# Waits per reader in place of the meetings of all engines between joint projection, SSD, RWKV and output projection; four SSD norm multiplications on GpSimd

## The reference, cut to what matters

```python
z, xbc, dt, rw, gq, gk, gv, gd, og = _split(u @ w_in, IN_WIDTHS)      # joint projection
xbc = silu(dwconv_centred(xbc))                                       # per channel, 3 taps
y = unboth(_ssd_chunked(both(xs, xs), both(dt_f, dt_b), ...))         # SSD, both directions
y = y + ssd_d[:, None] * xs
y_ssd = _rmsnorm_groups(y * silu(z), ssd_norm_w, 256)                 # SSD norm
kk = kk / jnp.maximum(jnp.sqrt(jnp.sum(kk * kk, -1)), 1e-12)          # RWKV preparation
y = unboth(_rwkv7_scan(both(r, r), both(w_f, w_b), ...))              # RWKV, both directions
y_rwkv = (layernorm_heads(y) * lnx_w + lnx_b + bonus) * gate
y_gla = ...
y_mix = jnp.concatenate([y_ssd, y_rwkv, y_gla], axis=-1)
return y_mix @ w_out                                                  # output projection
```

## Time and profile before

| | us |
|---|---|
| runs, median | 2151.59 |
| runs, lowest and highest of three | 2148.78, 2156.02 |
| the profiled execution, its own time | 2151.16 |
| its span, first to last instruction | 2149.0 |
| TensorE busy | 1929.7 |
| DVE busy | 1028.0 |
| ACT busy | 623.6 |
| GpSimd busy | 188.2 |

### The profile page before, as it was taken

How to read it: one execution, slowest core, us unless ns; L and a number is a source line. 1 busy time by engine, 2 the same in 40 slices (tenths; PEclk the granted TensorE clock), 3 DMA queues, 4 the chain that set the end, 5 groups by cost and what they waited for, 6 DMA issues and landing times.

```text
span 2149.0 us, 33639 instructions
## 1 busy us (share of the span) xinstructions
PE 1929.7 (90%) x14454; PEld 1401.6 (65%) x14454; DVE 1028.0 (48%) x1414; ACT 623.6 (29%) x917; POOL 188.2 (9%) x207
## 2 busy tenths in 40 slices
PE   6878999899996999899997669769899999999992
PEld 5758999889985999665755569665344444444440
DVE  4665555555555677645465674654222111121116
ACT  4334333444444433310142332121111112111110
POOL 0000000000000000011100004001112112121213
PEclk9878999999998999999897789679999999999996
DMA  9213555544443767445410000054999898998886
GB/s 321 99 59 128 186 185 183 167 157 138 157 144 102 284 235 253 134 163 177 128 59 3 12 2 4 26 234 170 391 379 380 344 384 348 378 384 346 333 342 245
DMA packets 191892, 438.67 MB, mean 204 GB/s; under 512 B 24208, under 2 KB 145552, under 8 KB 162448
## 3 DMA queue, kind: packets, MB, share of 16 engines
q1 hardware_dynamic: 156336, 352.02, 44.1%
q0 software_dynamic: 23040, 43.05, 5.9%
q10 hardware_dynamic: 12384, 41.69, 5.0%
HBM read 501.68 MB, written 26.21 MB: 246 GB/s over the span
## 4 chain that ended last, share of the span: by engine, by line
PE 80%; DVE 11%; ACT 4%; DMA 3%; issue 2%; SPq 0%; POOL 0%; ACTq 0%; DVEq 0%; POOLq 0%
PE psum L346 29%; PE psum L3207 15%; PE psum L3228 8%; PE psum L1574 7%; PE psum L3178 4%; PE psum L1581 2%; PE psum L2559 2%; ACT w_hi L412 1%; DMA mem<-in_exp_w_dram 1%; DMA mem<-in_na_w_qkv_dram 1%; DVE w_lo L417 1%; DVE mem L3328 1%; PE psum L2543 1%; PE psum L576 1%; PE psum L2968 1%
## 5 line engine op out<-in xcount | busy, mean ns | idle before, releaser
L417 DVE TENSOR_TENSOR w_lo<-mem,w_hi 128x2048 fp32r<-128x2048 f32 x126 | 288.4, 2291 | 271.3 <-ACT w_hi L412 268.7
L346 PE MATMUL psum<-x_hi,w_hi 128*128 128x256 f32 x1216 | 352.1, 290 | 4.6 <-DVE x_lo L563 4.6
L3207 PE MATMUL psum<-mem 128*64 128x512 f32 x1536 | 342.6, 599 | 9.5 <-DMA mem<-in_exp_w_dram 9.4
L346 PE MATMUL psum<-x_hi,w_lo 128*128 128x256 f32 x1216 | 346.2, 285 | 0.0
L346 PE MATMUL psum<-x_lo,w_hi 128*128 128x256 f32 x1216 | 345.4, 284 | 0.0
L412 ACT ACTIVATE w_hi<-mem 128x2048 fp32r<-128x2048 f32 x126 | 241.4, 1919 | 209.8 <-PE psum L346 190.8
L3207 PEld LDWEIGHTS psum<-mem 128*64 128x64 f32 x1536 | 110.8, 138 | 233.3 <-issue 214.8
L346 PEld LDWEIGHTS psum<-x_hi,w_hi 128*128 128x128 f32 x1216 | 236.0, 194 | 11.2 <-DVE w_lo L417 5.0
L346 PEld LDWEIGHTS psum<-x_lo,w_hi 128*128 128x128 f32 x1216 | 239.6, 197 | 0.7
L346 PEld LDWEIGHTS psum<-x_hi,w_lo 128*128 128x128 f32 x1216 | 238.3, 196 | 0.0
L3228 PE MATMUL psum<-mem 128*64 128x512 f32 x768 | 177.0, 603 | 1.2 <-DVE mem L3279 1.0
(11 more groups left out here) (485 smaller groups left out, 2899.6 us busy)
## 6 DMA issues: line engine op xcount, KB each, us to landing
mem<-in_exp_w_dram SPq DMA_DIRECT2D x192, 1024.0 KB
mem<-in_dil_w_qkv_dram SPq DMA_DIRECT2D x36, 1024.0 KB, 5.2
mem<-in_ada_w_dram POOLq DMA_DIRECT2D x48, 512.0 KB, 4.5
y_rows<-mem ACTq DMA_DIRECT2D x48, 512.0 KB
mem<-in_ffn_w_gate_dram SPq DMA_DIRECT2D x22, 1024.0 KB, 5.3
mem<-in_ffn_w_up_dram SPq DMA_DIRECT2D x22, 1024.0 KB, 5.4
mem<-in_ffn_w_down_dram SPq DMA_DIRECT2D x22, 1024.0 KB, 4.8
mem<-in_w_in_dram SPq DMA_DIRECT2D x13, 1024.0 KB, 5.7
```

The source lines that it names most:

```text
L346: ins = pe.matmul(out, lhs[a], rhs[b], start=start and k == 0, stop=stop and k == 2, **kw)
L417: dve.tensor_tensor(w_lo[n % SLOTS][:, 0, :], ring[:, n % SLOTS, :], w_hi_f[n % HI][:, 0, :], ALU.subtract).then_inc(S("w_split"), 1)
L3207: ins = pe.matmul(psum[r, up, :].rearrange("p (a n) -> p a n", a=2), xg[:, b % 2, c, x * P + 64 * e:x * P + 64 * e + 64], w_up[s][e][:, :, ...
```

## The change

The three meetings go. Instead, the instructions that need another engine's last work wait for that alone. The GpSimd program runs its parts without them. The four multiplications of the SSD norm go from DVE to GpSimd, whose result DVE waits for before it writes the end of RWKV. The scores of SSD go to bank 5. In ACT's program the root of the SSD norm and the load of `rk_masks` stand in the middle of `rwkv_prep_act`, and the three loads of the third meeting stand behind the first weight split. GpSimd's memset before the second FFN waits for `x_split` instead of `x_added`.

```diff
@@ wo_pe, wo_act
     def wo_pe(pe):
+        pe.wait_ge(S("gate_silu"), 4)
+        pe.wait_ge(S("rk_kr"), 3)
...
         hi_act(act, W_OUT)
+        act.wait_ge(S("rk_kr"), 3)
+        ln_load(act, 0)
+        act.dma_start(router_w, d["router_w_2"][0].rearrange("(p c) e -> p c e", p=P)).then_inc(S("router_in"), 16)
@@ block1_pool
-        pool.wait_ge(S("x_added"), NT * 3)
+        pool.wait_ge(S("x_split"), X_NO["ff1"] + KC)
         mod1_pool(pool)
@@ ssd_pe
-                ins = pe.matmul(bank(2, P, (2 * t + g) * P), xbcT[:, 4 + g, sd_tok(t)], xbcT[:, 6 + g, sd_tok(t)],
+                ins = pe.matmul(bank(5, P, (2 * t + g) * P), xbcT[:, 4 + g, sd_tok(t)], xbcT[:, 6 + g, sd_tok(t)],
...
+                if k == 0:
+                    pe.wait_ge(S("sd_turn_out"), 2 * t + 2)
                 pe.wait_ge(S("sd_xde_n"), m + 1)
...
             if k == 0:
+                pe.wait_ge(S("sd_turn_out"), 8)
                 rows(0)
@@ ssd_act
-        act.wait_ge(S("group_sums"), 2)
-        act.activation(stat[:, 1, 0:4], stat[:, 0, 0:4], ACT.Sqrt, scale=1 / 256, bias=ln_eps).then_inc(S("group_root"), 1)
@@ ssd_dve
+                else:
+                    dve.wait_ge(S("sd_turn_out"), 2 * t + 2)
                 xdt(t, dr, sd_xde[:, dr, :])
...
             if k == 0:
+                dve.wait_ge(S("sd_turn_out"), 8)
...
-            link(dve, "dve", dve.tensor_tensor(y, y, bank(5 + t), ALU.add))
+            dve.tensor_tensor(y, y, bank(5 + t), ALU.add).then_inc(S("sd_off"), 1)
+            dve.wait_ge(S("sd_off"), 5 + t)
...
-        dve.wait_ge(S("group_root"), 2)
-        link(dve, "dve", dve.reciprocal(stat[:, 3, 0:4], stat[:, 1, 0:4]))
+
+    def ssd_norm_pool(pool):
+
+        pool.wait_ge(S("sd_off"), 7)
         for t in range(NT):
-            y2 = y_mix[:, t, 0:512].rearrange("p (g e) -> p g e", g=2)
-            link(dve, "dve", dve.tensor_tensor(y2, y2, bc(stat[:, 3, 2 * t:2 * t + 2], 2, 256), ALU.mult))
-            link(dve, "dve", dve.tensor_tensor(y_mix[:, t, 0:512], y_mix[:, t, 0:512], vr("ssd_norm_w"), ALU.mult))
+            y, y2 = y_mix[:, t, 0:512], y_mix[:, t, 0:512].rearrange("p (g e) -> p g e", g=2)
+            link(pool, "pool", pool.tensor_tensor(y2, y2, bc(stat[:, 3, 2 * t:2 * t + 2], 2, 256), ALU.mult))
+            pool.tensor_tensor(y, y, vr("ssd_norm_w"), ALU.mult).then_inc(S("gate_silu"), 1)
@@ rwkv_prep_pe
+        pe.wait_ge(S("sd_off"), 5)
...
+        pe.wait_ge(S("sd_off"), 6)
         za(0)
@@ rwkv_prep_act
-        act.dma_start(rk_mask.rearrange("p d n i -> p (d n i)"), d["rk_masks"]).then_inc(S("rk_tri"), 16)
...
         act.activation(sq, psum[:, 4:6, :], ACT.Sqrt).then_inc(S("rk_norm"), 1)
+        act.wait_ge(S("group_sums"), 2)
+        act.activation(stat[:, 1, 0:4], stat[:, 0, 0:4], ACT.Sqrt, scale=1 / 256, bias=ln_eps).then_inc(S("group_root"), 1)
+        act.dma_start(rk_mask.rearrange("p d n i -> p (d n i)"), d["rk_masks"]).then_inc(S("rk_tri"), 16)
@@ rwkv_prep_dve
         link(dve, "dve", dve.reciprocal(sq, sq))
+        dve.wait_ge(S("group_root"), 2)
+        dve.reciprocal(stat[:, 3, 0:4], stat[:, 1, 0:4]).then_inc(S("sd_off"), 1)
@@ rwkv_end_dve
         dve.wait_ge(S("group_root"), 3)
+        dve.wait_ge(S("gate_silu"), 4)
...
-        link(dve, "dve", dve.tensor_tensor(y_mix[:, :, 512:768], yk, rk_g, ALU.mult))
+        dve.tensor_tensor(y_mix[:, :, 512:768], yk, rk_g, ALU.mult).then_inc(S("rk_kr"), 1)
@@ block2_pe, block2_act, block2_dve: each without its three calls
-        fence(pe, "mixed")
-        fence(pe, "ssd_done")
-        fence(pe, "rwkv_done")
@@ block2_act
-        ln_load(act, 0)
-        act.dma_start(router_w, d["router_w_2"][0].rearrange("(p c) e -> p c e", p=P)).then_inc(S("router_in"), 16)
@@ block2_pool
-        for n in FENCES:
-            if n == "mixed":
-                mixed_pool(pool)
-            if n == "rwkv_done":
-                rwkv_levels_pool(pool)
-            fence(pool, n)
+        mixed_pool(pool)
+        ssd_norm_pool(pool)
+        rwkv_levels_pool(pool)
```

More of the change, by code:

```diff
@@ L129, in weave_order @@
     return order
-FENCES = ["mixed",
-          "ssd_done", "rwkv_done"]
 SECOND_USE = {
@@ L372, in take @@
         return slot(n, c, w)
[L374 to L382, removed]
     links = {}
@@ L2175, in ssd_dve @@
                         link(dve, "dve", dve.tensor_tensor(sd_sc[:, dr, t, :, :],
-                                                           bank(2, 256, t * 256).rearrange("p (g i) -> p g i", g=2),
+                                                           bank(5, 256, t * 256).rearrange("p (g i) -> p g i", g=2),
                                                            bc(tri[:, dr, :], 1, 2), ALU.mult))
@@ L3364, in block2_act @@
         mixed_act(act)
-        fence(act, "mixed")
         ssd_act(act)
-        fence(act, "ssd_done")
         rwkv_prep_act(act)
@@ L3371, in block2_act @@
         rwkv_end_act(act)
-        fence(act, "rwkv_done")
-        ln_load(act, 0)
-        act.dma_start(router_w, d["router_w_2"][0].rearrange("(p c) e -> p c e", p=P)).then_inc(S("router_in"), 16)
         wo_act(act)
@@ L3389, in block2_dve @@
         mixed_dve(dve)
-        fence(dve, "mixed")
         ssd_dve(dve)
-        fence(dve, "ssd_done")
         rwkv_prep_dve(dve)
@@ L3397, in block2_dve @@
         rwkv_end_dve(dve)
-        fence(dve, "rwkv_done")
         wo_dve(dve)
```

## The result

| | before | changed |
|---|---|---|
| median of five runs, us | 2151.59 | 2136.75 |
| lowest and highest | 2148.02, 2156.02 | 2132.64, 2138.69 |
| profiled execution, its time and span | 2151.16, 2149.0 | 2136.75, 2134.9 |

The changed kernel is faster by 14.8 us: the ratio is 0.9933, with a 95% interval from 0.9917 to 0.9948. In two later sets of runs it was 0.9949 twice (intervals 0.9931 to 0.9967 and 0.9936 to 0.9962), or 12.9 and 12.1 us. The forecast was 8.2 us.

A forecast was written before the change was run, and what follows sets the result against it. TensorE, busy 90% of the span, was taken as the bound, with time won only where it waits for a late engine. 3.25 + 0.4 + 6.5 - 0.2 - 4.2 + 2.45 = 8.2 us gave 2143.4 us, range 2137.0 to 2149.0.

The forecast's parts named there:

- memset: Norm before the second FFN: GpSimd's memset no longer stretches DVE's first row scaling; gain 3.25 us, bounds 2.5 and 3.3.
- first meeting: Joint projection to SSD: TensorE's state products start earlier, without DVE's drain and wake-up; gain 0.4 us, from 0 to 1.0.
- second meeting, less a reciprocal: SSD to RWKV: transposes start earlier, gain 6.5 us (worst 2.5, best 7.8); DVE's kept reciprocal costs 0.2.
- GpSimd beside DVE: RWKV preparation: four norm multiplications on GpSimd block DVE's chain; cost 4 x 1.06 = 4.2 us, from 0 to 5.3.
- third meeting, start: RWKV to output projection: weight split done earlier, first matmul waits for the 16 transposes alone; gain 2.45 us.
- third meeting, clock in transposes and matmuls: Output projection: 1.2 us lost if the clock rises when it did, 1.5 won if 4.7 us after the start.
- four doors: DVE's RWKV preparation chain: semaphore waits behind its instructions let GpSimd in four times, at 1.06 us each.
- No blocking: Rival: GpSimd does not block DVE in the RWKV preparation; 4.2 us more gained, 2139.2 us; chance 0.15.
- Nothing net: Rival: RWKV's start gains 2.5 us at the half clock, blocking costs 5.3; 2148.5 us; chance 0.12.
- Waits without effect: Rival: DVE bounds the stretch, so only the memset's move counts; 2148.3 us; chance 0.08.
- slower: Rival: the output projection starts earlier but stays at the half clock; 2161.9 us; chance 0.04.

The follow-up runs named there:

- memset alone: Kernel before with only the memset's wait changed from `x_added` to `x_split`; 2150.72 us against 2152.41, ratio 0.9992.
- memset back: Changed kernel with GpSimd's memset again waiting for the sixth `x_added`; 2141.91 us against 2150.92 before, ratio 0.9959; a second, single execution 2147.06 us.
- first meeting back: Changed kernel with only the meeting of four engines behind the joint projection put back; a single execution took 2140.77 us.
- second meeting back: Changed kernel with only the meeting behind SSD put back; 2142.63 us against 2150.92 before, ratio 0.9965.
- norm later: Changed kernel with GpSimd's four norm multiplications held until `rk_bonus`; 2132.04 us, ratio 0.9921 to before; again 2136.66 us beside the changed kernel's 2136.10.
- half later: Changed kernel with GpSimd's two norm multiplications of the second row tile held until `rk_bonus`; a single execution took 2130.91 us.
- third meeting back: Changed kernel with the meeting before the output projection and ACT's old order (loads before weight split) put back; 2143.59 us against 2150.92 before, ratio 0.9963.

## Why the prediction was right, and where it was not

Forecast 2143.4 us, measured 2136.75: faster, as said, by 6.6 us more than said, and 0.25 us below the low end of the range. By its terms, against the first profile:

| term | forecast | measured | shown by |
|---|---|---|---|
| memset | 3.25 | 3.25 | memset alone, memset back |
| first meeting | 0.4 | 0 (0.26 at 36 us, lost behind) | first meeting back |
| second meeting, less a reciprocal | 6.3 | 8.0, 7.1 or 5.5 | second meeting back, the clock |
| GpSimd beside DVE | -4.2 | -3.1 | norm later, half later |
| third meeting, start | 2.45 | 2.5 | third meeting back |
| third meeting, clock in transposes and matmuls | 0 | 0.6 or 1.9 | stages d and e |
| sum | 8.2 | 11.3 or 12.7, with 8.0 for the second meeting | |

**Memset**: right in place and size. The row of the same norm without GpSimd was the whole argument.

**First meeting**: the step "L2124 starts at 1165.68 and could at about 1165.3" held (0.38 us earlier), but I put the 0.4 in the sum. DVE was 0.26 us ahead at 36 us and lost it in one wait for products that ran at a lower clock. A start moved earlier is no gain before the end is followed.

**Second meeting**: the mechanism held row by row (transposes ahead of the sum, products at once, the same 7.95 us to the root). Mis-sized was the clock, in its place and its price: I let it rise 3.2 us behind the last square sum and took 7.0 us for that. It rose before it (two profiles of the changed kernel), some 6 us behind it (one, and still 7.2 us gained), or 9 to 10 us behind it (memset back and first meeting back). My 6.5 lies between the 5.6 and the 8.1 that came out, "at best 7.8" was too tight by 0.3, and "at worst 2.5" was far too low: with the clock up only 9 to 10 us behind the sum the gain was still 5.6.

**GpSimd beside DVE**: four doors, as predicted, but 0.8 us each and not 1.06, the price of the one L2605 in the earlier trace rows. The Trainium skill (SBUF — State Buffer, section "SBUF: two separate sides") says that whichever of the two engines starts first holds the shared port pair for its whole instruction, and that the other is blocked until then. The runs agree: half the work cost half, GpSimd waited as well, and none of the four stretched DVE instructions ended before the GpSimd instruction that it met. The product (1237.54 + 1.94 = 1239.48) ended 1.08 us behind L2241 (1237.18 + 1.22 = 1238.40), the copy (1240.91) 0.29 behind L2242 (1240.62), where they take 1.23 and 0.43 alone. What was mis-sized is the wait: I charged DVE with nearly a whole GpSimd instruction each time (1.06 of 1.27), while it paid what was left of one that had begun before, less some 0.2 us.

**Third meeting**: right for the start. The term for the clock was put at nothing, with bounds of 1.2 and 3.9 around the whole. It gave 0.6 or 1.9 us on top, inside the upper bound in one profile (3.1) and beyond it in two (4.5).

**The rivals.** *No blocking* named a time of 2139.2, the nearest to what was measured, and its mechanism is the one that the norm later refutes: near in number, wrong in cause. *Nothing net* is wrong: the start of RWKV gave 5.0 us net of blocking with the early clock, 2.5 with the late one. *Waits without effect* and *slower* are wrong: stage b fell, and the matmuls of the output projection got shorter.

**What the sum can't hold**: 11.2 of the 14.1 us between the two profiles lie in edited stages; the other 2.9 are the balance of stages with the same code (1.58 ahead of the first edit, 1.34 before the levels, -2.64 in levels and scan, 2.58 in the experts). The medians, 12.1 to 14.8 us, are near the 11.3 to 12.7 of the terms. Single ends of single executions would have told anything from 5.4 to 17.7: the spans of the three profiles of the changed kernel are 2134.9, 2143.6 and 2131.3.

## What to carry to other kernels

A meeting of all engines costs what the early engines could have done before the last one came. Look at the first instructions behind it on the longest chain: the first of these three cost 0.3 us at most, although TensorE waited 7.8 us at it, the second 3.4 us at the low clock, the third 2.5, and this last, it seems, for an order of instructions on ACT. Work handed from DVE to GpSimd is not off the path while DVE runs a chain of copies, scalings and two-input products in SBUF: here four instructions of 0.69 us on DVE turned into 3.1 us of stretching. Let them wait for a place where DVE waits itself. And settle changes of 0.1% by stages of the trace, since the ends moved by 12 us between executions of one program; take the stage in front along, as a clock that rises late in one may have been up for longer in the other.

## What the runs showed of the hardware

**The place where TensorE's clock rises differs between executions of one program, and is worth more than some edits.** In the same kernel the 9 us from the last square sum ran at 1.00 or 0.68 (13.28 or 14.22 us to the bound under the root), and at 0.50 in two variants (15.8). The 168 matmuls of the output projection took 19.8 or 20.8 us in profiles of the same kernels. The Trainium skill (TensorE: Matmul & The Clock Gate, Part 1) says that the number of matmuls at the low clock varies from run to run of one kernel, and puts the loss at under 1% of a typical span. The runs agree that it varies: over five executions of the changed kernel the mean granted clock lay between 0.930 and 0.937 and the time between 2132.64 and 2138.69 us, 0.3%. What the low clock costs in all, no run here shows. A spread of 0.3% is as much as the changes under test.

**DVE and GpSimd side by side in SBUF both pay.** DVE lost 3.1 us and GpSimd 2.0 in the same stretch. A DVE product that ran when GpSimd began kept its 1.20 us, and GpSimd's first instruction took 1.93 us in place of 1.04; the next DVE pair took 2.56 in place of 1.13. Beside DVE instructions that read PSUM (the first masks of the RWKV products, with GpSimd's four beside them in the second run of the norm later) GpSimd kept 1.04 and 1.27 us.
